# A one-core decoder step: dense blocks placed between the parts of the mLSTM scan and of its sample heads, and the sample heads put on row and column groups of TensorE

## What is computed

```
u = x * (1 + scale(c)) + shift(c)
z, xbc, dt, q, k, v, ig, fg, og, up, gl = split(u @ w_in)
y_ssd  = rms_norm(ssd_scan(conv(xbc), dt) * silu(z))           # branch 0
h      = mlstm_scan(q, k, v, ig, fg, C, n, m)                  # branch 1
y_m    = head_norm(h) * mlstm_norm_w * sigmoid(og)
y_pool = pool_mix(up)                                          # branch 2
g = sigmoid(gl + gate_b)                                       # three gates
merged = g[0]*(y_ssd @ w_br_ssd) + g[1]*(y_m @ w_br_mlstm) + g[2]*(y_pool @ w_br_pool)
x = layer_norm(ALPHA*x + (1+gate(c)) * (merged @ w_out))
x = layer_norm(ALPHA*x + (1+gate_f(c)) * mixture_of_experts(x))

mlstm_scan, for a chunk of 128 prompt tokens (or the 4 of a sample) and each of 4 heads of 256:
  wts = exp(dmat - m) * (q @ k.T);  ws = exp(m_st - m)
  num = wts @ v + ws * (C @ q);     den = wts.sum + ws * (n . q)
  h   = num / max(|den|, exp(-m))
  C   = wprev*C + (wsrc*v).T @ k;   n = wprev*n + (wsrc*k).sum
```

## Time and profile before

| | us |
|---|---|
| median of 3 runs | 1594.39 (1592.38 to 1595.14) |
| the profiled execution, its time | 1596.01 |
| its span in the profile | 1594.2 |
| PE busy | 1434.9 (90% of the span) |
| DVE busy | 485.6 (30%) |
| ACT busy | 235.4 (15%) |
| POOL busy | 146.4 (9%) |
| mLSTM, from its first transpose to the first matmul of gate1 | 866.5 to 1067.2 |

### The profile page before, as it was taken

How to read it: one execution, slowest core, us unless ns; L and a number is a source line. 1 busy time by engine, 2 the same in 40 slices (tenths; PEclk the granted TensorE clock), 3 DMA queues, 4 the chain that set the end, 5 groups by cost and what they waited for, 6 DMA issues and landing times.

```text
span 1594.2 us, 15623 instructions
## 1 busy us (share of the span) xinstructions
PE 1434.9 (90%) x6485; PEld 1058.1 (66%) x6485; DVE 485.6 (30%) x962; ACT 235.4 (15%) x338; POOL 146.4 (9%) x197
## 2 busy tenths in 40 slices
PE   5899899999999999999999888979999745999945
PEld 3688688878778887778877555558878532444423
DVE  0636325545352000000000775750111450111136
ACT  1122111121110000000011222001001330112103
POOL 1000007920000000000000001200000013000020
PEclk9999999999999999999999998989999976999977
DMA  9421211112431222324242001821130152899841
GB/s 392 175 80 53 59 67 43 55 54 96 156 133 57 76 80 94 144 109 156 106 157 107 27 1 36 296 93 62 71 133 3 79 214 80 320 346 363 301 152 56
DMA packets 30403, 202.43 MB, mean 127 GB/s; under 512 B 3896, under 2 KB 4280, under 8 KB 16248
## 3 DMA queue, kind: packets, MB, share of 16 engines
q1 hardware_dynamic: 17568, 148.86, 25.3%
q0 software_dynamic: 12768, 52.61, 9.1%
HBM read 169.80 MB, written 32.02 MB: 127 GB/s over the span
## 4 chain that ended last, share of the span: by engine, by line
PE 80%; DVE 9%; DMA 6%; ACT 2%; issue 2%; POOL 1%; SPq 0%; POOLq 0%; DVEq 0%; ACTq 0%; PEldq 0%
PE PS L520 53%; PE PS L977 5%; PE PS L995 3%; PE PS L886 2%; PE PS L891 2%; DMA ring<-in_wstream 2%; DMA proj<-in_wexp 2%; DMA ring<-in_wexp 2%; PE PS L549 1%; PE PS L627 1%; PE PS L918 1%; PE PS L637 1%; PE PS L666 1%; PE PS L834 1%; PE PS L559 1%
## 5 line engine op out<-in xcount | busy, mean ns | idle before, releaser
L520 PE MATMUL PS<-uT,ring 128*128 128x272 f32 x2688 | 631.4, 395 | 7.1 <-ACT proj L1108 6.8
L520 PEld LDWEIGHTS PS<-uT,ring 128*128 128x128 f32 x2688 | 510.7, 191 | 118.0 <-ACT proj L1108 7.2
L520 PE MATMUL PS<-proj,ring 128*128 128x272 f32 x768 | 178.9, 393 | 0.0
L520 PEld LDWEIGHTS PS<-proj,ring 128*128 128x128 f32 x768 | 145.5, 190 | 31.8 <-issue 2.0
L1325 DVE TENSOR_TENSOR adaM<-PS,V 128x144 f32<-128x144 f32 (+1 forms) x2 | 0.5, 270 | 297.3 <-PE PS L559 297.3
L1444 DVE TENSOR_TENSOR gs<-gs,PS 128x544 f32<-128x544 f32 x16 | 11.6, 722 | 211.7 <-PE PS L520 211.7
L977 PE MATMUL PS<-proj,work 128*128 128x512 f32 x160 | 70.7, 595 | 2.6 <-DMA proj<-in_wexp 2.5
L520 PE MATMUL PS<-merged,ring 128*128 128x272 f32 x256 | 59.3, 393 | 1.8 <-DVE merged L1446 1.8
L520 PEld LDWEIGHTS PS<-merged,ring 128*128 128x128 f32 x256 | 48.6, 190 | 12.1 <-DVE merged L1446 2.2
L977 PEld LDWEIGHTS PS<-proj,work 128*128 128x128 f32 x160 | 29.6, 190 | 37.0 <-issue 35.1
L1137 ACT ACTIVATE gs<-PS,V 128x544 f32<-128x544 f32 x24 | 17.1, 714 | 228.3 <-PE PS L520 228.2
(11 more groups left out here) (403 smaller groups left out, 1468.5 us busy)
## 6 DMA issues: line engine op xcount, KB each, us to landing
ring<-in_wstream SPq DMA_DIRECT2D x83, 1024.0 KB, 4.9
proj<-in_wexp SPq DMA_DIRECT2D x10, 3072.0 KB, 12.8
ring<-in_wexp SPq DMA_DIRECT2D x6, 3072.0 KB, 12.0
expert_rows<-proj SPq DMA_DIRECT2D x16, 512.0 KB, 12.6
proj<-in_caug POOLq DMA_DIRECT2D x12, 514.0 KB, 6.3
out_cm_s<-proj POOLq DMA_DIRECT2D x12, 514.0 KB, 4.3
expert_rows<-proj POOLq DMA_DIRECT2D x1, 4096.0 KB, 13.3
proj<-in_ssd POOLq DMA_DIRECT2D x4, 1024.0 KB, 11.4
```

What stands on the lines that cost most here:

```text
L520: last = mm(acc(mi)[:, h, :], wblk(b % RING, kt, mi), rhs[:, kt, h * HALF:(h + 1) * HALF], start=kt == 0, stop=kt == KT - 1)
```

## The change

Four things change together.

1. **The order of the weight stream.** After br2 the 12 blocks of k, v and q come at once, with the 16 ada blocks among them (some in pairs). The 16 blocks gate0/br0 (8), og (4) and gate1 (4) form a list `FILL` and run inside the mLSTM stage. Only br1 and out stay behind it.
2. **The scan.** It is given banks 4 to 7 alone. `fill(n)` issues n units of `FILL`; a unit is one `kt` step of a half, 2 matmuls, and 16 units are a block. Each step has fill(2), scores, fill(6), `ml_mid`, states of the first head, fill(4), states of the second head, fill(4), `ml_back`, and then the front of the next step. `keep_warm` is gone. With four banks alone, the front of step s+1 now comes behind the back of step s.
3. **The sample heads.** They run one head after another. The tokens are replicated to four groups of 32 partitions (`krep`, `vrep`); the four matmuls with the old state of a part go to four column groups, their results lie on four groups of partitions, are copied by ScalarE (`nb`) and added up by a matmul with `fold`. Each state contribution uses one row group and takes one of three banks in turn; from the third on, a fill(1) follows each. A head has fills of 6, 14 (one at a time), 7 and 2 units. 3 units stand between scan and heads, 9 behind them.
4. **Small things that follow.** og is multiplied in later (per tile and head, on VectorE), the sigmoids of og and of gate1 are kept in `proj`, the SSD merge is done between VectorE's parts of the scan, `CB` has 6 buffers instead of 10 and the first two are loaded earlier.

The core of the diff:

```diff
+QKV = (4, 5, 6, 7, 8, 9, 10, 11, 0, 1, 2, 3)
+FILL = ([x for i in range(4) for x in (("gate0", i), ("br0", i))] + [("qkvo", 12 + i) for i in range(4)]
+        + [("gate1", i) for i in range(4)])
+STEP_FILL = (2, 6, 4, 4)
+AFTER_SCAN, HEAD_FILL = 3, (6, 14, 7, 2)
...
-            merge(0, proj[:, 12:20, :], br_ready, 1)
-            for i in range(16):
+            for n, i in enumerate(QKV):
                 dense_block("qkvo", i, uT)
-                ada_block(N_ADA_FIRST + i)
...
             ml_front(0)
             for s in range(NS):
+                fill(STEP_FILL[0])
+                ml_scores(s)
+                fill(STEP_FILL[1])
                 ml_mid(s)
+                ml_states(s, 0)
+                fill(STEP_FILL[2])
+                ml_states(s, 1)
+                fill(STEP_FILL[3])
+                ml_back(s)
                 if s + 1 < NS:
                     ml_front(s + 1)
-                ml_back(s)
+            fill(AFTER_SCAN)
...
+                mm(PS[0:L, 4, 0:257], Ems[0:L, :], vs[0:L, :], start=True, stop=False)
+                for q in range(4):
+                    i, k, jh = 4 * h + q, q // 2, q % 2
+                    pe.wait_ge(caug_moved[i % NCB], 32 * (i // NCB) + 16)
+                    for r in range(4):
+                        last = mm(PS[32 * r:32 * r + 32, 4, 0:257], qm[:, k, 4 * jh + r, :], CB[i % NCB][:, r, :],
+                                  start=r > 0 and q == 0, stop=q == 3, tile_position=(0, 32 * r))
...
+                    for r in range(4):
+                        m = 4 * q + r
+                        if m >= 3:
+                            pe.wait_ge(ml_upd, u0 + m - 2)
+                        mm(PS[:, 5 + m % 3, 0:257], km[32 * r:32 * r + 32, jh, k * P:(k + 1) * P], vs[32 * r:32 * r + 32, :],
+                           start=True, stop=True, tile_position=(32 * r, 0)).then_inc(ml_st, 1)
+                        if m >= 2:
+                            fill(1)
+                pe.wait_ge(ml_nb, h + 1)
+                mm(PS[0:L, 4, 0:257], cc("fold"), nb, start=True, stop=True).then_inc(ml_num, 1)
...
             for h in range(4):
+                n, hs = NS + h, hstat[:, 0:32]
+                sample_inputs(h)
+                sample_states(h)
+                head_outputs(n, L, h, 1, 4, c, hs)
+                dve.wait_ge(og_ready, 2 * h + 2)
+                do(v.tensor_tensor(proj[:, 2 * h, 0:TP], proj[:, 2 * h, 0:TP], proj[:, 12 + 2 * h, 0:TP], ALU.mult))
+                head_norm(n, L, h, 1, hs)
```

More of the change, by code:

```diff
@@ L41 @@
          + [("br2", 1), ("gate2", 2), ("br2", 2), ("gate2", 3), ("br2", 3)]
-         + [x for i in range(4) for x in (("gate0", i), ("br0", i))]
-         + [x for i in range(16) for x in (("qkvo", i), ("ada", N_ADA_FIRST + i))]
-         + [x for i in range(4) for x in (("gate1", i), ("br1", i))] + [("out", i) for i in range(4)])
+         + [x for n, i in enumerate(QKV) for x in [("qkvo", i)] + [("ada", N_ADA_FIRST + k) for k in ada_beside(n)]]
+         + FILL + [("br1", i) for i in range(4)] + [("out", i) for i in range(4)])
 MERGES = (2, 0, 1)
@@ L778, in _, with fill @@
             ada_fold(N_ADA - 1)
             pe.wait_ge(ada_ready, 2)
-            accs_emptied("gate1")
             pe.wait_ge(evac_qk, 24)
-            def keep_warm(bank, n):
-                for _ in range(n):
-                    mm(PS[:, bank, :], ident, C[:, 0:512], start=True, stop=True)
+            filled = [0]
+            def fill(n):
+                for u in range(filled[0], filled[0] + n):
+                    (name, i), mi, kt = FILL[u // 16], u // 8 % 2, u % 8
+                    if (name, i, mi, kt) == ("br0", 0, 0, 0):
+                        pe.wait_ge(br_ready, 1)
+                    dense_part(name, i, proj[:, 12:20, :] if name == "br0" else uT, mi, kt, kt + 1)
+                filled[0] += n
@@ L801, in ml_front @@
                 for i in range(4):
[L802 removed]
+                    last = nc.tensor.transpose(PS[:, 5, i * P:(i + 1) * P], proj[:, qkv_tile(16 + 4 * g + i), cols], ident)
                 last.then_inc(ml_kv, 1)
+                for r in range(2):
+                    for j in range(2):
+                        last = mm(PS[:, 7, (2 * r + j) * P:(2 * r + j + 1) * P], row4(2 * g + j),
+                                  G[64:68, 3 + 2 * r, cols], start=True, stop=True)
@@ L806, in ml_front @@
                         t = 2 * (2 * g + j) + k
[L807 to L811, removed]
+                        last = mm(PS[:, 6, j * P:(j + 1) * P], proj[:, qkv_tile(8 + t), cols], proj[:, t, cols],
+                                  start=k == 0, stop=k == 1)
                 last.then_inc(ml_sc, 1)
@@ L868, in _ @@
[L868 to L878, removed]
@@ L904, in _ @@
+            for h in range(4):
+                sample_head(h)
+            fill(16 * len(FILL) - filled[0])
+            pe.wait_ge(ml_out, NS + 4)
+            for i in range(4):
+                dense_block("br1", i, proj[:, 0:8, :])
             pe.wait_ge(gate_used, 24)
```

386 lines of the change are left out of this document (202 added, 184 removed).

## The result

The changed kernel takes **1522.4 us** (median of 4 runs, 1519.2 to 1523.8) against 1593.4 us of the kernel before in the same comparison (4 runs, 1591.4 to 1595.1). The ratio is 0.9546, with a 95% interval of 0.9531 to 0.9560. The forecast was 1529.5 us with a range of 1505 to 1552. The profiled execution has a span of 1522.0 us, 72.2 less than before.

A forecast was written before the change was run, and what follows sets the result against it. TensorE was taken to bound the kernel, with waits for VectorE's norm and identity matmuls in the mLSTM stage. Seven terms summed to 373 us against 437.8, a gain of 65: 1594.39 - 65 = 1529.5 us, range 1505 to 1552.

The forecast's parts named there:

- What bounds the kernel: Whole kernel: TensorE busy 90% of the span; only less work for it or fewer holes in it help.
- term 1: mLSTM stage: the 16 dense blocks of `FILL` are still issued, 234.7 us.
- terms 2 and 3: Scan: its own matmuls, 59.0 us, and seams between dense pieces and small matmuls, 3.2 us.
- term 4: Sample heads: their own matmuls, including trips to row groups and column-group rounds, 71 us, bounds 41 and 91.
- term 5: Start of the mLSTM stage: time lost to a low granted clock, 3 us, bounds 0 and 4.3.
- terms 6 and 7: Replicating sample tokens before the first head, 1.3 us left uncovered, and late norms in the scan, 0.5 us.
- The cover: Scan step: VectorE's chain of 8.5 to 9.0 us fits barely under 9.1 us of TensorE work.
- Cheap trips: Heads and seams: single contributions slip between dense units with hardly a gap; gain 98, about 1497 us; chance 0.16.
- Late chains: Scan and heads: VectorE misses its cover or column groups do not overlap; 1545 to 1565 us; chance 0.13.
- The clock in the heads: Sample heads: small stops bring the granted clock to 0.64, 100 us more, 1629 us; chance 0.03.
- The size: Whole kernel: the gain from the change, 437.8 us of the same work falling to 373, 65 us.

The follow-up runs named there:

- Experiment 1: Changed kernel with no dense units inside the sample heads: og blocks run ahead of the heads, gate1 blocks behind; 1567.7 us.
- experiment 6: Changed kernel with no dense unit and no merge inside the scan; the eight gate0/br0 blocks run behind it; 1620.1 us.
- Experiment 2: Changed kernel with old-state matmuls one after the other into the same 32 partitions instead of on four column groups; 1542.0 us.
- experiment 3: Changed kernel with contributions in groups of three, then three dense units, and old-state rounds in two pairs; 1493.3 us.
- Experiment 9: Changed kernel with contributions in groups of three and the scan's first two dense units moved ahead of the wait for the conditioning; 1488.8 us.
- experiment 4: Changed kernel with a scan step's units as 4, 6, 3, 3 instead of 2, 6, 4, 4; 1526.3 us.
- experiment 7: Kernel before the change, without its identity matmuls and nothing else changed; 1606.4 us.

## Why the prediction was right

**What bounds the kernel.** Right. The stage ran on TensorE and on its waits for VectorE's norm. Experiments 1 and 6 show the dense work as cover: 45 us in the heads, 98 in the scan. They need not add up to the gain, since the bare scan and the bare heads are also worse than those before.

**The dense blocks, term 1, and the scan's matmuls, terms 2 and 3.** From 689.79 to the first head at 875.06 it took 185.3 us; 131 units, 59.0 of own work, the seams, the clock, 1.3 and 0.5 had given 187.1. The step was to be 22.5 and was 22.48. The seams were over-priced: three of four dense pieces in a step cost what their units cost, and only the one behind the gate rows costs 0.20 more, 1.6 in eight steps where 3.2 were taken. The own work of that step is 22.48 - 14.87 = 7.6, where 7.8 was taken.

**The heads, term 4.** Forecast 71 us, measured 67.7: from 875.06 to 1047.23, the end of the last transposes, it took 172.2 us, less 114 units at 0.917. This is the largest miss of a term. A trip came at 0.82 instead of 0.835; the round of old states cost 0.57 where 0.635 was taken, and the small matmuls of a head's front 1.3 with 0.2 behind them, where 1.7 had both. The forecast distance of 1.75 from one contribution to the next was met by 1.74. Experiment 2 confirms the price of the column groups, experiment 3 that of a trip.

**The clock, term 5.** 3 us were taken, with 4.3 as the upper bound, and that was too little. From the first transposes (689.79) to the second dense piece (699.33) it took 9.5 us; the same matmuls in the third step take 4.9 (735.96 to 740.84). So the low clock cost 4.7 us. The wait that the prediction named is still there at 1.3 us. Experiment 9 took both away. That the part ahead of the heads came out within 2 us of the forecast is in part luck: the clock cost 1.7 us more, the seams 1.6 and the own work some 1.4 less.

**Waits, terms 6 and 7.** Forecast were 1.3 and 0.5 us; PE's waits show 0.7 and 0.3.

**The cover.** VectorE's chain in the odd steps had been put at 8.5 to 9.0 us under 9.1 of cover, "barely". It has nothing to spare. The odd steps are those with a half merge, the second, fourth, sixth and eighth. These are rows of DVE and PE in the sixth, and two of DVE in the eighth:

```profile
821.61 1.00 DVE L1722 SCALAR_TENSOR_TENSOR work<-work,wpb,PS 128x257 f32<-128x257 f32 x2 [0.46 <-PE PS L864]
...
824.04 0.72 DVE L1515 TENSOR_TENSOR merged<-merged,gs 128x544 f32<-128x544 f32 x1 [0.50 <-DVE gs L1513]
...
825.89 0.63 PE L872 MATMUL PS<-C,xs 128*128 128x128 f32 x4 [0.28 <-DVE xs L1712]
...
867.06 1.00 DVE L1722 SCALAR_TENSOR_TENSOR work<-work,wpb,PS 128x257 f32<-128x257 f32 x2 [0.46 <-PE PS L864]
...
869.98 0.86 DVE L1712 TENSOR_SCALAR xs<-xs 128x256 f32<-128x256 f32 x2
```

In the eighth step the norm ends at 870.84 and PE's back starts at 870.98; the same 0.14 us lie between the two in the sixth step, where PE waited. The chain is longer than in experiment 4 because VectorE has to wait 0.46 us for the second head's states, which stand behind four units here and behind three there. In the sixth step VectorE idles 0.50 us between the merge's two instructions, for a reason that no run here shows, and TensorE waits 0.28. So the chain was on the edge in the odd steps, and the forecast of hardly a wait held by a few tenths of a microsecond.

**The rivals.** Cheap trips: no, a trip costs what was read; but experiment 3 shows that fewer trips give as much as this rival promised (1493 us against its 1497). Late chains: no wait in the heads, 0.3 us in the scan. The clock in the heads: 1.00. It was the right thing to fear, though. Experiment 1 has the same small matmuls without the dense units, and there the granted clock is 0.56. What holds it up in the changed kernel is the dense work itself. In the scan before the change the identity matmuls did, as experiment 7 shows, and their removal alone loses 12 us.

**The size.** The gain was put at 65 and is 71 by the medians. Of the 6, 5.1 are in the stage (3.3 in the heads, 1.8 ahead of them), the rest is outside it. TensorE's busy share was to be near 91.5% and is 91.5%.

## What to carry to other kernels

Where a chain over the small engines sets the pace, look for matmuls elsewhere that need nothing of it. Cut them into pieces as long as each link of the chain, count link against cover in rows of the trace, and move what may come late (here half a merge) behind the link for which TensorE waits. Pay for a change of the array's tiling once per group and not once per matmul: three contributions on three row groups cost as much as one, and grouping them gave 29 us on top of 71. Work that only keeps the engine awake can be worth its time; take it out only when useful work takes its place.

## What was not expected of the hardware

Identity matmuls that fill a wait paid for themselves: without them the same kernel is 12 us slower, and a numerator behind a rest of 4.7 us ran at a granted clock of 0.50 (5.1 us for 2.6). Yet the same means did not hold the clock in the bare heads (0.82 with eleven of them a head). With two dense units, 1.9 us, in place of one wait of 1.3 us the granted clock was 1.00 from 684 to 696 us, where it had been 0.70.
